# Sparse attention placed between the weight units of its query projection and of the output's first pair, and the cross attentions' norms one unit earlier

## The reference

```
proj = h @ w_in                       # q 16x128, k 128, v 128, qi 16x64, ki 64, wi 16
q, k, qi, ki = rope(...)              # each
rel = relu(einsum('bqhd,bsd->bqhs', qi_b, ki))
iscore = einsum('bqh,bqhs->bqs', wi_b, rel), causal
idx = top_k(iscore, 64)
logits = q . k at idx * 128 ** -0.5;  p = softmax(logits);  out = p . v at idx
x = x + out @ w_out
x = x + cross(rms_norm(x, norm_xattn[i]), memn, ...)   # 4 heads of 128
x = x + swiglu(rms_norm(x, norm_ffn[i]), ...)
```

## Time and profile before

| what | us |
|---|---|
| median of 3 runs | 3070.36 (3069.67 to 3071.99) |
| the profiled execution | 3070.45 |
| its span, first to last instruction | 3068.7 |
| TensorE busy | 3021.8 (98%) |
| VectorE busy | 1701.0 (55%) |
| ScalarE busy | 1480.0 (48%) |
| GpSimd busy | 227.3 (7%) |
| mean granted TensorE clock | 0.997 of full |

### The profile page before, as it was taken

One profiled execution on the slowest core, in us unless ns is written; L12 is line 12 of the kernel. 1 busy time (PEld: TensorE's weight loads), 2 busy tenths in 40 slices (PEclk: granted clock), 3 DMA queues, 4 the chain that ended last, 5 costly groups with the idle time before them and its releaser, 6 DMA issues.

```text
span 3068.7 us, 38273 instructions
## 1 busy us (share of the span) xinstructions
PE 3021.8 (98%) x14184; PEld 2491.0 (81%) x14184; DVE 1701.0 (55%) x1802; ACT 1480.0 (48%) x1835; POOL 227.3 (7%) x221
## 2 busy tenths in 40 slices
PE   8999999999999989999999999999999999999999
PEld 7788888888888768888888888888887888888787
DVE  5664544544456855644454545457555555755654
ACT  6554444444445454554444434455555545455553
POOL 0110000000000220100000000004300000510000
PEclk9999999999999999999999999999999999999999
DMA  7666666666666526666666666666544556644455
GB/s 249 220 188 187 191 190 187 190 186 192 192 195 185 154 79 193 200 190 187 190 190 187 190 190 189 190 197 191 151 144 138 155 181 179 185 148 147 139 157 171
DMA packets 280736, 549.44 MB, mean 179 GB/s; under 512 B 16897, under 2 KB 18977, under 8 KB 280225
## 3 DMA queue, kind: packets, MB, share of 16 engines
q1 hardware_dynamic: 276352, 531.30, 57.8%
q0 software_dynamic: 4256, 16.40, 1.5%
HBM read 540.82 MB, written 6.82 MB: 178 GB/s over the span
## 4 chain that ended last, share of the span: by engine, by line
PE 91%; DVE 4%; ACT 3%; DMA 1%; issue 1%; SPq 0%; ACTq 0%; DVEq 0%
PE ps L442 23%; PE ps L931 21%; PE ps L495 12%; PE ps L450 11%; PE ps L938 10%; PE ps L470 6%; DVE w_lo L387 1%; PE ps L1158 1%; PE ps L1069 1%; ACT w_hi L380 1%; PE ps L765 1%; PE ps L1136 1%; PE ps L1046 1%; PE ps L905 1%; DMA w_raw<-xattn_w_kv 1%
## 5 line engine op out<-in xcount | busy, mean ns | idle before, releaser
L387 DVE TENSOR_TENSOR w_lo<-w_raw,w_hi 128x1024 fp32r<-128x1024 f32 x1008 | 1269.8, 1261 | 1310.1 <-ACT w_hi L380 1306.1
L380 ACT ACTIVATE w_hi<-w_raw 128x1024 fp32r<-128x1024 f32 x1008 | 1067.5, 1060 | 1473.1 <-PE ps L450 621.0
L931 PE MATMUL ps<-w_hi,actT_hi 128*128 128x512 f32 x1408 | 550.0, 391 | 0.0
L931 PE MATMUL ps<-w_hi,actT_lo 128*128 128x512 f32 x1408 | 547.9, 389 | 0.0
L938 PE MATMUL ps<-w_lo,actT_hi 128*128 128x512 f32 x1408 | 376.5, 389 | 0.0
L495 PE MATMUL ps<-w_hi,actT_hi 128*128 128x512 f32 x832 | 336.5, 404 | 5.7 <-ACT pall L519 5.7
L495 PE MATMUL ps<-w_hi,actT_lo 128*128 128x512 f32 x832 | 325.4, 391 | 0.0
L442 PE MATMUL ps<-w_hi,hidT_hi 128*128 128x512 f32 x864 | 319.5, 391 | 0.0
L938 PEld LDWEIGHTS ps<-w_lo,actT_hi 128*128 128x128 f32 x1408 | 264.3, 188 | 55.1
L931 PEld LDWEIGHTS ps<-w_hi,actT_lo 128*128 128x128 f32 x1408 | 264.4, 188 | 54.2
L931 PEld LDWEIGHTS ps<-w_hi,actT_hi 128*128 128x128 f32 x1408 | 264.3, 188 | 54.1
(11 more groups left out here) (297 smaller groups left out, 2909.9 us busy)
## 6 DMA issues: line engine op xcount, KB each, us to landing
w_raw<-ffn_w_in SPq DMA_DIRECT2D x352, 512.0 KB, 3.7
w_raw<-w_in SPq DMA_DIRECT2D x256, 512.0 KB, 3.6
w_raw<-ffn_w_out SPq DMA_DIRECT2D x176, 512.0 KB, 4.7
w_raw<-w_out SPq DMA_DIRECT2D x64, 512.0 KB, 3.7
w_raw<-attn_w_in SPq DMA_DIRECT2D x48, 512.0 KB, 3.7
w_raw<-xattn_w_kv SPq DMA_DIRECT2D x32, 512.0 KB, 6.4
w_raw<-attn_w_out SPq DMA_DIRECT2D x32, 512.0 KB, 4.1
w_raw<-xattn_w_q SPq DMA_DIRECT2D x16, 512.0 KB, 3.8
```

The source lines that it names most:

```text
L380: nc.scalar.activation(w_hi[:, v % NS], w_raw[:, v % NS], ACT.Copy).then_inc(w_hi_done, 1)
L387: nc.vector.tensor_tensor(w_lo[:, v % NS], w_raw[:, v % NS], w_hi[:, v % NS].bitcast(F32), ALU.subtract).then_inc(w_lo_done, 1)
L931: nc.tensor.matmul(ps[:, 2 * b + tb], lhs[:, k, tb * P:(tb + 1) * P], w_hi[:, s, kk * CB:(kk + 1) * CB], start=(k == 0 and part == 0), sto ...
```

## The change

What it does, in order of the diff:

- `qiT`, `kidup`, `ixr`, `isc`, `isw` and `zero` move to other places in memory.
- `aq0` and `aq1` become one product `aq` of four blocks that goes by rows, on accumulator halves 1, 0, 1, 0. `xq1`'s and `v1`'s halves change with it.
- In the output's first pair the units come in the order: block 0's 0 to 3, block 1's 0 to 3, 4 and 5 of each, 6 and 7 of each. SyncE loads in that order too. Block 0's transposes are paid at unit 7.
- The two cross attentions' norms: squares at 1 and 2 instead of 2 and 3, root at 4 instead of 5, variance at 3 instead of 4, scales at 5 instead of 6.
- The attention units run behind positions 15 to 42 (`pe_dsa`, and with the same tables `act_dsa` and `dve_dsa`, the exponentials one position behind the scores); each has a query job of its own, four transposes and a copy of 512 columns instead of eight and 1024 for a pair.
- The index jobs stand behind positions 1, 2, 3 and 5, index scores behind 3 to 10, selection steps behind 11 to 21.
- VectorE rotates only the index keys; GpSimd rotates keys and index queries in three parts, and the queries by half groups, from the eighth index sum on.

```diff
@@ -284,8 +285,7 @@
         add("akv_end", wv(a["attn_w_in"][0]), [full], 1, lambda i: (6 * CB,), 1, ATTN_IN - 6 * CB)
-        add("aq0", wv(a["attn_w_in"][0]), [full] * 2, 1, lambda i: (0, CB))
-        add("aq1", wv(a["attn_w_in"][0]), [full] * 2, 1, lambda i: (2 * CB, 3 * CB))
+        add("aq", wv(a["attn_w_in"][0]), [full] * 4, 1, lambda i: (0, CB, 2 * CB, 3 * CB), 4)
         add("aout", wv(a["attn_w_out"][0]), [full] * 2, 2, two)
@@ -307,11 +307,12 @@
         ROWS, n_rows = {}, 0
-        for name in ("xq0", "k1", "xq1", "v1", "rest0", "rest1"):
+        for name in ("xq0", "k1", "aq", "xq1", "v1", "rest0", "rest1"):
             ROWS[name] = n_rows
...
-        ROWS_HALF = dict(xq0=0, k1=1, xq1=0, v1=1, rest0=0, rest1=0)
+        ROWS_HALF = dict(xq0=(0,), k1=(1,), aq=(1, 0, 1, 0), xq1=(1,), v1=(0,), rest0=(0,) * NREST, rest1=(0,) * NREST)
@@ -321,6 +322,14 @@
+        def units_of(name, i):
+            li = L[name]
+            if name == "aout" and isinstance(i, int) and i == 0:
+                return [(b, j) for part in ((0, 1, 2, 3), (4, 5), (6, 7)) for b in range(2) for j in part]
+            return [(b, j) for b in range(li.per_pair) for j in range(li.units)]
@@ -387,47 +395,51 @@
+        def turn_at(name, i, b):
+            return 7 if name == "aout" and i == 0 and b == 0 else 1
...
-                for b in range(li.per_pair):
-                    for j in range(li.units):
-                        us = li.u0 + b * li.units + j
-                        last = evac and j == li.units - 1
-                        if isinstance(i, int):
-                            split(eng, us + i * li.body)
-                        else:
-                            split(eng, us, i, li.body)
-                        if mid:
-                            mid(i, b, j)
-                        pay(who, j)
-                        if last:
-                            evac(i, b, li.u0 + (b + 1) * li.units + i * li.body)
-                    if turn_x:
-                        owed[who].append((1, lambda i=i, b=b: turn_x(i, b)))
+                for t, (b, j) in enumerate(units_of(name, i)):
+                    us = li.u0 + t
+                    last = j == li.units - 1
+                    if isinstance(i, int):
+                        split(eng, us + i * li.body)
+                    else:
+                        split(eng, us, i, li.body)
+                    if mid:
+                        mid(i, t // li.units, t % li.units)
+                    pay(who, j)
+                    if evac and last:
+                        evac(i, b, us + 1 + i * li.body)
+                    if turn_x and last:
+                        owed[who].append((turn_at(name, i, b), lambda i=i, b=b: turn_x(i, b)))
...
@@ -589,7 +604,8 @@
-            at_ = dict(mem=(5, 6, 7), mix0=(1, 2, 4), final=(1, 2, 3), in0=(4, 5, 6)).get(name, (2, 3, 5))
+            at_ = dict(mem=(5, 6, 7), mix0=(1, 2, 4), xattn0=(1, 2, 4), xattn1=(1, 2, 4), final=(1, 2, 3),
+                       in0=(4, 5, 6)).get(name, (2, 3, 5))
             return [(at_[0], lambda: squares(0)), (at_[1], lambda: squares(1)), (at_[2], root)]
@@ -645,6 +661,8 @@
                 return [(6, variance), (7, scales)]
+            if name.startswith("xattn"):
+                return [(3, variance), (5, scales)]
             return [(4, variance), (6, scales)]
@@ -1206,45 +1227,63 @@
-        def pe_attend(pe, units):
...
+        DSA_JOB = (15, 20, 22, 23, 26, 27, 34, 36)
+        DSA_SCORED = (16, 21, 24, 25, 27, 29, 35, 37)
+        DSA_SHARED = (18, 24, 26, 27, 29, 31, 37, 39)
+        DSA_TURNED = (21, 26, 28, 29, 31, 34, 39, 41)
+        DSA_VALUED = (22, 27, 29, 30, 32, 35, 40, 42)
+        DSA_BANK = (0, 0, 2, 2, 2, 2, 4, 4)
+        def pe_dsa(pe, pos_):
+            units = stages["dsa"]
+            for n, un in enumerate(units):
+                if pos_ == DSA_JOB[n]:
+                    pe.wait_ge(ix_relu, 8)
+                    turned = sum(s < pos_ for s in DSA_TURNED)
+                    if turned:
+                        pe.wait_ge(pt_copied, units[turned - 1]["n"] + 1)
+                    if n == 7:
+                        pe.wait_ge(sc_read, units[6]["n"] + 1)
+                    pe_job(pe, un["new"][0], psum=4)
+            for n, un in enumerate(units):
+                if pos_ == DSA_SCORED[n]:
+                    if n in (0, 2):
+                        for tb in range(TB):
+                            pe.wait_ge(row_free[tb], ROWS["aq"] + 2 + n // 2)
+                    pe_scores(pe, un)
+                if pos_ == DSA_TURNED[n]:
+                    pe.wait_ge(qt_copied, units[sum(j <= pos_ for j in DSA_JOB) - 1]["jobs"])
+                    if n == 6:
+                        pe.wait_ge(sc_read, units[7]["n"] + 1)
+                    pe_probs(pe, un)
+                if pos_ == DSA_VALUED[n]:
+                    pe_shared_values(pe, un)
...
@@ -1278,22 +1317,26 @@
...
-                job = new_job([(ain[:, h, (4 * g + k) * P:(4 * g + k + 1) * P], k * SEQ + h * P)
-                               for k in range(4) for h in range(TB)], flat(qkT[:, g % 2]), 1024)
-                job["turned"] = g + 1
...
+                    job = new_job([(ain[:, tb, (4 * g + k) * P:(4 * g + k + 1) * P], k * P) for k in range(4)],
+                                  qkT[:, g % 2, :, tb * P:(tb + 1) * P], 512)
+                    job["turned"] = 2 * g + tb + 1
...
-                    out.append(new_unit(True, keys=nk, jobs=job["n"] + 1, new=[job] if tb == 0 else [], row=None,
+                    out.append(new_unit(True, keys=nk, jobs=job["n"] + 1, new=[job], row=None, bank=DSA_BANK[2 * g + tb],
@@ -1678,9 +1721,7 @@
             dve.wait_ge(proj_done, PROJ["akv_end"])
-            yield from rope_heads(ain, QI0, 16, 64, cos_of(64, 96), sin_of(64, 96))
-            yield from rope_heads(ain, KI0, 1, 64, cos_of(64, 96), sin_of(64, 96))
-            yield from rope_heads(ain, K0, 1, P, cos_of(0, 64), sin_of(0, 64))
+            yield from rope_heads(ain, KI0, 1, 64, cos_of(64, 96), sin_of(64, 96), (tmpA, tmpA[:, 1024:2048]))
             for q in range(2):
@@ -1688,18 +1729,17 @@
+        IX_JOB = {1: 0, 2: 1, 3: 2, 5: 3}
+        IX_AT = 3
...
@@ -1755,15 +1797,31 @@
+        SELECTED = {11: 2, 12: 2, 13: 2, 14: 2, 15: 1, 16: 1, 17: 2, 18: 1, 19: 2, 20: 1, 21: 2}
...
-            pool.wait_ge(nat_done, 1)
-            for half in range(2):
-                pool.wait_ge(proj_done, PROJ[f"aq{half}"])
-                for g in (2 * half, 2 * half + 1):
-                    for _ in rope_heads(ain, 4 * g * P, 4, P, cos_of(0, 64), sin_of(0, 64), (ropeA, ropeB),
-                                        eng=nc.gpsimd, mark=plink, link=plink):
-                        pass
+            def turn(c0, heads, hd, lo, hi, halves=range(TB)):
+                for _ in rope_heads(ain, c0, heads, hd, cos_of(lo, hi), sin_of(lo, hi), (ropeA, ropeB), halves,
+                                    eng=nc.gpsimd, mark=plink, link=plink):
+                    pass
+            pool.wait_ge(acc_free[0], half0["akv"][0] + 1)
+            turn(K0, 1, P, 0, 64)
+            turn(QI0, 4, 64, 64, 96)
+            pool.sem_inc(i_turned, 1)
+            pool.wait_ge(acc_free[1], half0["akv"][1] + 1)
+            turn(QI0 + 256, 8, 64, 64, 96)
+            pool.sem_inc(i_turned, 1)
+            pool.wait_ge(proj_done, PROJ["akv_end"])
+            turn(QI0 + 768, 4, 64, 64, 96)
+            pool.sem_inc(i_turned, 1)
+            pool.wait_ge(ix_added, 8)
+            for g in range(4):
+                for tb in range(TB):
+                    pool.wait_ge(row_free[tb], ROWS["aq"] + g + 1)
+                    turn(4 * g * P, 4, P, 0, 64, (tb,))
                     pool.sem_inc(q_turned, 1)
@@ -2037,12 +2095,22 @@
-            pe_linear(pe, "aq0", *xT, t_lo_done, ready_of("mix1"), mid=lambda i, b, j: pe_index(pe, 8 * b + j))
-            pe_linear(pe, "aq1", *xT, t_lo_done, ready_of("mix1"),
-                      mid=lambda i, b, j: pe_index(pe, 16 + 8 * b + j))
-            pe.wait_ge(proj_done, PROJ["aq1"])
-            pe.wait_ge(nat_done, 2)
-            pe_attend(pe, stages["dsa"])
+            dsa = stages["dsa"]
+            def aq_begin(e):
+                if e == 3:
+                    pe.wait_ge(sc_read, dsa[1]["n"] + 1)
+            def in_aq_pe(pos_):
+                pe_index(pe, pos_)
+                pe_dsa(pe, pos_)
+            pe_rows(pe, "aq", *xT, t_lo_done, ready_of("mix1"), mid=in_aq_pe, begin=aq_begin)
+            def aout_begin(b):
+                if b == 0:
+                    pe.wait_ge(sc_read, dsa[5]["n"] + 1)
+                for tb in range(TB):
+                    pe.wait_ge(row_free[tb], ROWS["aq"] + 3 + b)
@@ -2207,24 +2276,15 @@
-            index_in = dsa_index_in(dve)
-            def in_aq0(i, b, j):
-                if b == 0:
-                    beside(index_in, 3)
-                dve_index(dve, 8 * b + j)
```

(26 more changed lines are left out.)

223 lines of the change are left out of this document (104 added, 119 removed).

## The result

| | before | after |
|---|---|---|
| median, us | 3070.02 (3069.12 to 3071.99, 4 runs) | 3050.74 (3048.87 to 3054.66, 4 runs) |
| ratio, 95% interval | | 0.994 (0.9928 to 0.9951) |
| profiled execution / its span | 3070.45 / 3068.7 | 3052.06 / 3050.2 |
| mean granted clock | 0.997 | 0.999 |

The change gains 19.3 us by the medians. The forecast was 3048.5 with 3045 to 3057: 2.2 too low, and inside the range.

The account below looks back on a forecast made before the run. TensorE was taken as the bound, with 52.6 us lacking weight units. 52.6 + 0.8 - 29.7 - 2.6 - 0.7 + 1.6 = 22.0 us gained, from 3070.45 to 3048.5 us, range 3045 to 3057.

Parts of the forecast that it names:

- The stage without weight units: Between query projection and output: 52.6 us of sparse attention alone removed, 29.7 us of inserted groups added between units.
- The index wait: Before the first index job: TensorE's 0.8 us wait for VectorE goes, and small index-query rotations cost nothing.
- Own copies: At positions 26 and 34 TensorE waits for ScalarE's copy of the query job just issued: 1.3 us each, 2.6 together.
- Row wait at 24: Scores at position 24 wait for ScalarE's late eviction, held behind VectorE's maximum of unit 1: 0.7 us, bounds nothing and 2.
- VectorE, 1.6 to spare: End of unit 11 to start of unit 24: VectorE needs 36.7 us where TensorE takes 38.3, so no wait.
- Selection beside GpSimd: VectorE's selection steps during GpSimd's rotations: assumed not slowed; bounds nothing, or some 12 steps doubled, 10 us.
- Rival (1): VectorE late: selection suffers beside rotations, or more own-copy waits; 4 to 9 us given back, 3052.5 to 3057.5; chance 0.22.
- The rule weighed: Shared-port lock of VectorE and GpSimd: at worst eight w_lo each wait one full rotation, some 2 us worse, about 3050.5.
- rival (2): The port costs a whole rotation each time: eight w_lo wait 0.8 instead of 0.42, giving 3050.5 us; chance 0.08.
- GpSimd as a cliff: Half-group query rotations cost nothing at 6.2 us; from 12 they eat the gain, at 13 about 3080; chance 0.03.
- The norms: First cross attention: norms one unit earlier remove TensorE's 1.6 us wait; in the second, nothing gained.
- no copies are waited for: Rival in which all copy waits are hidden: 3045.2 us, the floor; counted within the forecast's own chance of 0.60.

Follow-up runs that it names:

- fix_index: Changed kernel with only the third index-query job moved from position 3 to position 4: 3050.88 us, 0.9936 of before.
- fix_all: Changed kernel with three orders mended together (own bank for two query jobs, third index job later, unit 1's exponentials behind the eviction): 3046.38 us, 0.9922 of before.
- pool_plus6: Changed kernel with six more unused GpSimd operations ahead of each half group of query rotations: 3079.99 us, 1.0036 of before.
- pool_plus2: Changed kernel with two more unused GpSimd operations ahead of each half group of query rotations: 3058.61 us, 0.9964 of before.
- norms_back: Changed kernel with the cross attentions' norms back at their old place, one unit later: 3052.65 us, 0.9945 of before.
- select_heavy: Changed kernel with selection steps finding their eight maxima twice, adding VectorE work: 3056.50 us, 0.9958 of before.
- before_warm: Kernel before the change with 20 unused filler products in TensorE's 4.65 us wait ahead of the sparse attention: 3067.07 us, 0.999 of before.
- fix_copies: Changed kernel with only the query jobs of units 4 and 6 in a bank of their own, probabilities awaiting earlier copies alone: 3050.53 us, 0.9939 of before.
- attend_alone: Changed kernel with the sparse attention back in one block behind the query projection, index work staying early: 3063.89 us, 0.9977 of before.

## Why the prediction was right, and where 2.2 us went

- **The stage without weight units, 52.6 for 29.7.** Right. The 52.6 hold some 5.6 of low clock, by the slices, which went with them. Between the marks the sum with its waits was 52.6 + 0.8 - 29.7 - 2.6 - 0.7 = 20.4, measured 18.06. The inserted groups cost what the rows said: after a job of four the next unit's first product comes 0.35 later and that product takes 0.1 more (0.45 in the sum), scores over 256 keys pitch at 1.54 and lengthen the next by 0.2 (1.73), and the clock beside them is 1.00.
- **The index wait, 0.8 gained.** Wrong, the largest miss of this stage. The step was "small rotations ... I price them at nothing and leave 3 us of room": that was an estimate for the job at position 1 only. The job at position 3 waits for the third part of GpSimd's work, which ended 0.9 late. The second part (958.52 to 975.15 on GpSimd's timeline) held it up: eight of its twelve operations of 256 columns took 1.6 beside VectorE's work instead of 0.74, some 7 us more. The third part started right behind it, at 975.33, and three of its operations of 128 columns took 1.32 instead of 0.46. Of the 3 us of room, 1.0 was left at position 1 (the job starts at 976.10). A wait for VectorE was replaced by one for GpSimd: 0.9, shown by fix_index, which gains 1.03. (The expectation of fix_index names the second part; the trace row, L1819, is the third.)
- **Own copies, 2.6.** Right in place and cause, 1.26 twice by the wait rows; within fix_all the mended order accounts for 2.9 (4.92 less 1.03 and 0.99), 0.3 above the forecast. What the 0.4 beyond the two waits consists of is not shown.
- **Row wait at 24, 0.7.** Right: 0.58 in the row, and 0.99 comes back between the marks when the exponentials stand behind the eviction, some 0.1 of it at position 25 (0.51 for 0.65).
- **VectorE, 1.6 to spare.** Right for the place that the ledger ends at: the read of unit 1's scores ends at 1052.44 and unit 24 starts at 1053.49, 1.05 later. But that was not the nearest due date. The row wait at 24, which the prediction prices by itself, hangs on the maximum right behind that read, and on that chain VectorE had nothing to spare (0.58 of waiting). The ledger also has nine selection steps a half at 0.72 and 0.98, where eight search and the ninth writes the mask, and eight w_lo delayed by 0.42, where it was 0.29 in the mean; these err to the safe side. And it stopped at position 24, where the prediction missed a term: at 25 unit 3's scores go into the bank of unit 2's, which VectorE reads behind a w_lo, 0.65 of waiting and some 0.8 with what surrounds it.
- **Selection beside GpSimd.** Right for its main steps: MAX8 at 420 and 423 ns with and without rotations. Rival (1)'s doubling did not happen, except for the two small operations named above.
- **The rule weighed.** The eight w_lo beside rotations took 1.51 in the mean and 1.79 at most, against 1.22 without rotations: a delay of 0.29 in the mean, and of 0.57 at most, never a rotation of 0.74. GpSimd's own operations of 256 columns took 0.74 or so when free and mostly 1.5 to 1.8 when delayed. The Trainium skill (SBUF — State Buffer, section SBUF: two separate sides) says that the second to start blocks until the first is through; the rows agree with that if the delay is only what is left of a running instruction. Reading it as a whole instruction each time, as rival (2) did, is what the rows speak against, and the time of 3050.7 near rival (2)'s 3050.5 is a coincidence of other terms.
- **GpSimd as a cliff.** Right that it was far: no wait for it in the query rotations at 5.8 to 7.6 per half group, 7.0 in the mean (6.2 was forecast). pool_plus6, at 13, is slower than the kernel before. The ledger misses the clock behind a long wait and the later maximum at 24, for which pool_plus2 pays 1.7 each of its 7.8.
- **The norms, 1.6.** Too much: 0.93 less waiting in the row of this one profile, 0.4 against norms_back, at most 0.6 in the time. The step "One unit earlier removes the cause" was right; that nothing else would be late behind it was not, and "cover: weights ahead" was wrong: the weights were the next to be late.

The miss adds up: index 0.9, position 25 0.8 and copies 0.3 make 2.0 of the 2.3 between the marks (20.4 less 18.06); the last 0.3 is not assigned. Ahead of them 0.44 was gained instead of 1.6, which makes 1.2 more, and the spans' difference came to 18.5 where 22.0 was forecast. The medians put the difference at 19.3, as the changed kernel's profiled execution was 1.3 above its median.

**What won.** fix_all is the fastest kernel of this study: 3046.38, 0.9922 of before. It leaves one wait of 0.47 in the stage, so at 1.2 above the forecast's floor of 3045.2 ("no copies are waited for") little is left in this idea.

## What to carry to other kernels

When a stage with small operations is spread between units of a saturated engine, what it gains can be read beforehand as stage length less the inserted operations' own time. Here that was 22.9; the 18.06 measured, with the waits of the new order added back (0.9, 0.7, 0.8 and 2.9) and the old 0.8 taken off, make 22.6. The rest is a list of single waits, each read from the order of one helper engine: follow every shared bank to its next user, and make the ledger of each engine to every place where it is due, not to the one that looks tight. Mend such waits together: one alone can only move the wait to the next late engine, and each was smaller than what the runs could tell.

## What the hardware showed that I had not expected

- A long wait of TensorE is not only its own length, and what it costs on top hardly grows with it. By the slices of 1 us the low clock behind single waits of 2.46 (select_heavy), 3.62 (pool_plus2), 4.24, 7.41, 5.35 and 5.06 (pool_plus6) cost 1.7, 1.7, 1.7, 2.2, 1.9 and 2.1 us. Between weight units, waits of up to 1.55 left the granted clock at 1.00; in before_warm's block without units it fell behind four waits of 0.73 to 1.11.
- One reason why runs of one kernel spread. Behind the second mark, with the same work, the profiled spans have 1893.6 us (fix_copies, pool_plus6), 1895.1 to 1895.3 (before, after and six others) or 1896.9 (attend_alone, norms_back, fix_index), in steps of about 1.65. In the second half of the program TensorE twice waits 2.3 us for VectorE, near 2320 and 2840; behind each the clock falls in some executions and not in others, and the three lengths go with no fall, one and two. The stretch in fix_index and in fix_copies:

```profile
2838.00:2846.00 8.00, 6.17 (x24) 5.26 (x25) 6.29 (x7) 1.75 (x3) 0.00 (x0) 0.79 0.52 160
```

```profile
2836.00:2844.00 8.00, 6.35 (x38) 5.68 (x39) 6.03 (x7) 3.11 (x4) 0.00 (x0) 1.00 0.50 148
```

  A difference of 1.65 or 3.3 between two runs can be this alone (what makes the rest of the widest spread, 6.6 in norms_back, is open), so single waits of under 2 us are judged by marks around them, not by times.
- Filler products in the 4.65 us of idle time in front of a stage of small operations gave back 2.3 to 2.8 us, with the clock of the stretch behind them at 0.86 for 0.72.
- VectorE's and GpSimd's delays beside each other are lopsided by kind. Two-input operations from SBUF are delayed on both (w_lo 1.22 to 1.51 in the mean, a rotation of 256 columns 0.74 to 1.6, one of 128 columns 0.46 to 1.32), and so was one VectorE operation with a single input (TENSOR_SCALAR, 0.22 to 0.75). MAX8, MATCH_REPLACE8 and the read from PSUM (L1104, 0.69) were not.
